# Stick-breaking scores in three rounded passes, and the order of a step around them

## The chip, the cores and the metric

One core of a Trainium2 chip runs the whole program. The metric is device time in microseconds (us), the median of several runs. The engines are TensorE (PE; its weight loads are shown apart as PEld), VectorE (DVE), ScalarE (ACT), GpSimdE (POOL) and SyncE (SP), which issues the DMAs.

## The reference

One layer on x (1 x 1024 x 1024, float32). An input projection to 5,376 columns gives q, k, v and gates of two mixers and two merge gates. Mixer A is a sliding-window attention with sinks and rotary positions. Mixer B is stick-breaking attention with 8 heads of 64 dimensions, strictly causal:

```python
z = jnp.einsum('bhtd,bshd->bhts', q_blk, k).astype(jnp.float32) * (D ** -0.5)
causal = kpos[None, :] < qpos[:, None]
log_keep = jnp.where(causal, -jax.nn.softplus(z), 0.0)
between = lax.cumsum(log_keep, axis=3, reverse=True) - log_keep
w = jnp.where(causal, jnp.exp(jax.nn.log_sigmoid(z) + between), 0.0)
return jnp.einsum('bhts,bshd->bhtd', w.astype(v.dtype), v)
```

Each mixer's output is gated with SiLU and projected up; both are merged with sigmoid gates, go through an output projection, and a LayerNorm of 1.189 x + that follows. The diff touches the first einsum (the scores z), the buffers around it and the order of the work.

## The kernel before, in words

**Products.** Features lie on partitions, time (backwards) along the free axis. Every large matrix product is made in float32r: each operand is split into a rounded part `hi` (an ACT copy into a float32r tile) and the rest `lo` (a DVE subtraction, original minus hi), and `mma3` (L214 to L216) adds three matmuls, hi by hi, hi by lo and lo by hi. The input projection has 20 pairs of weight tiles with 7 products each (`N_PRODUCTS` is 140; product q belongs to pair q // 7, position q % 7), each product being 12 matmuls of 128x128 by 128x512 into PSUM bank q % 2. Products of the later pairs are the filling between other work. After product q, ACT reads the bank (`read_bank`, L807 or L812) and rounds weights for a product three or four ahead (`part_high`, L717); DVE adds blocks (`add_block`, L1118: positions 1, 4, 5), forms sums of weights (L1127 to L1134: positions 4 and 5, two operations each) and subtracts the low parts (`low_part`, L1138: two at position 0, none at 5, one elsewhere). So a position decides how much DVE does after it: 2, 2, 1, 1, 4, 3, 1 operations for positions 0 to 6.

**Steps.** Mixer B runs in 20 steps, 5 to each pair of heads. Step s takes one or two tiles of 128 queries (`parts(s)`) that fill 1,024 score columns for each head (512 in the fifth step of a pair, which is called j = 4 below; the steps of a pair are j = 0 to 4). In PSUM the scores are four banks, z. The columns are cut where a bank ends: runs of 512+512 columns for j = 0, 512+384+128 for j = 1, 512+256+256 for j = 2, 512+128+384 for j = 3, 512 for j = 4. Key and query tiles of a pair are `ks` and `qs`, written by products well ahead.

PE's order in step s (L1612 to L1630): `values(s-2)` (L1605), `scores(s)` (L1578, float32 matmuls, one head in partitions 0 to 63 and the other in 64 to 127), `turn(s-1)` group 0 (transposes of the weights, L1593), a product, groups 1 and 2, half a product, group 3, the other half, in j = 0 the transposes of v (`turn_values`, L1559), and a third product except in j = 4.

The other engines follow with semaphores, each in its own written order. ACT: `keeps(s)` (L984, sigmoids of z; waits for the scores and for values(s-2)), copies of the turned blocks (L964), bank reads and weight roundings, and `betas(s)` (L992), which waits for the last transposes of s-1 and reads z for the last time; `scores(s+1)` waits for it. POOL cuts the diagonals (L662, L667). DVE: `gated_out(s-2)` (L1299), a scan over the first head (`break_sticks`, L1280), what follows the first product, the scan over the second head, what follows the second product, `weigh(s)` (L1288; its first piece releases group 0 of the next step's transposes), and what follows the third.

SP loads weights and stores gates and outputs. Everything else of the kernel (mixer A in a window stage before, up projection, output projection, LayerNorm behind) is not touched but for buffers and the semaphores that guard them.

Of the kernel before, what the change touches and what calls it, by code (L numbers as in the profile page):

```python
# [13 lines left out]
P = 128  # L14
SEQ = 1024
# [33 lines left out]
STEP_0 = 42  # L49
# [52 lines left out]
def halves_done(n, h):  # L102

    return 2 * h + n + 1

# [113 lines left out]
def build(nc, xt, xn, w, bias, cos, sin, sinks, ln_g, ln_b, out):  # L219
    with ExitStack() as ctx:  # L220
# [53 lines left out]
        with ExitStack() as b:  # L274
            keep0 = sb("keep0", [P, 2, SEQ], F32, b)
            keep1 = sb("keep1", [P, 2, SEQ], F32, b)
            beta = sb("beta", [P, 2, SEQ], F32, b)
            sig_g = sb("sig_g", [P, 2, HALF], F32, b)
            o_b1 = sb("o_b1", [P, SEQ], F32, b)
            v_n1 = sb("v_n1", [P, SB, P], F32, b)  # L280
            ks0, qs0 = sb("ks0", [P, SEQ], F32, b), sb("qs0", [P, SEQ], F32, b)
            v_n0 = sb("v_n0", [P, SB, P], F32, b)
            qs1, ks1 = sb("qs1", [P, SEQ], F32, b), sb("ks1", [P, SEQ], F32, b)
        qs, ks, v_n, o_b = (qs0, qs1), (ks0, ks1), (v_n0, v_n1), (o_b0, o_b1)
        keep = (keep0, keep1)

# [86 lines left out]
        def block_at(sp, m, nh):  # L373


            if sp in Q_PAIRS:
                return qa[sp][:, 8 * nh:8 * nh + 8, m, :]
            if sp in G_PAIRS:
                slot = GATE_SLOT[m, nh]
                return gate_st[:, slot, :] if slot < 2 else sw[:, slot - 2, :]  # L380
            if sp >= MG_PAIR:
# [39 lines left out]
        z_done, keep_set, beta_set = sem("z_done"), sem("keep_set"), sem("beta_set")  # L421
        keep_cut, beta_cut, scanned, w_ready = sem("keep_cut"), sem("beta_cut"), sem("scanned"), sem("w_ready")
# [34 lines left out]
        def _(sp):  # L457
# [41 lines left out]
            def merge_gate_store(i, m, nh):  # L499
                at = 4 * (i % 2) + 2 * m + nh  # L500
                if (m, nh) == (1, 0):
                    sp.wait_ge(bank_read, NP * i + 7)
                else:
                    sp.wait_ge(block_sig, 3 * (i - MG_PAIR) + BLOCKS.index((m, nh)) + 1)
                sp.dma_start(sig_d[i - MG_PAIR, m][:, half(nh)], sig_m[:, at, :]).then_inc(sig_out[at], 16)
# [12 lines left out]
            def gate_back(a):  # L518
                if a == 0:
                    for slot in GATE_SLOT.values():  # L520
                        sp.wait_ge(gate_out[slot], 16 * len(G_PAIRS))
                else:
                    sp.wait_ge(ga_set, a)
                sp.dma_start(v_t[:], gate_d[a]).then_inc(gate_in, 16)
# [160 lines left out]
        def _(act):  # L685
# [62 lines left out]
            def room(i, pos):  # L748
# [15 lines left out]
                for p in range(PAIRS):  # L764
                    if i == pair_kq(p) and pos == 0:
                        if p == 0:
                            act.wait_ge(rope_done, len(ROPE_ORDER))
                            for m in range(2):
                                act.wait_ge(gate_out[GATE_SLOT[m, 1]], 16 * len(G_PAIRS))
                        else:  # L770
                            act.wait_ge(za_done, twos)
                            if p >= 2:
                                act.wait_ge(z_done, PER_PAIR * (p - 1))
                    if i == pair_vg(p):
# [12 lines left out]
                if i == MG_PAIR and pos == 0:  # L787
                    act.wait_ge(z_done, PER_PAIR * (PAIRS - 1))
                if i == MG_PAIR + 1:
                    if pos == 0:  # L790
                        act.wait_ge(o_done, PER_PAIR * (PAIRS - 1))
                    if pos == 4:
                        act.wait_ge(z_done, STEPS)
# [27 lines left out]
            def gate_a_sigmoid(a):  # L821
                act.wait_ge(gate_in, 16 * (a + 1))
                if a == 0:
                    act.wait_ge(ob_out, 16 * (PAIRS - 1))
                else:
                    act.wait_ge(ga_mul, a)
# [28 lines left out]
            def gate_b_sigmoid(p):  # L855

                i = pair_vg(p)
                for h in range(2):
                    wait_block(act, i, 1, h)
                    if p == 0 and h == 0:  # L860
                        for k in range(2):
                            act.wait_ge(oa_out[k], 16 * NCHUNK // 4)
                    if p > 0:
                        act.wait_ge(gate_set, 2 * (p - 1) + h + 1)
                    act.activation(sig_g[:, h, :], o_b[p % 2][:, half(h)], ACT.Sigmoid).then_inc(gate_sig, 1)
# [51 lines left out]
            act.wait_ge(t_lo[4], 2)  # L917
            def exponents(c):
# [29 lines left out]
            for c in range(NCHUNK + 5):  # L948
                if c % 2 == 0 and c >= 6:
                    turned_chunk(c - 5)  # L950
                after(WINDOW_1 + c)
                if c % 2 == 0 and 4 <= c < NCHUNK + 4:
                    turned_chunk(c - 4)
                if c < NCHUNK:
                    exponents(c)

# [10 lines left out]
            def turned_values(p):  # L967

                if p == 1:
                    act.wait_ge(gate_out[GATE_SLOT[1, 0]], 16 * len(G_PAIRS))  # L970
                for g in range(2):
                    at = RING_AT["v", p, g]
                    act.wait_ge(turned, ring_count(at, False) + 1)
                    act.activation(v_n[p % 2][:, 4 * g:4 * g + 4, :].rearrange("p a d -> p (a d)"),
# [79 lines left out]
        def _(dve):  # L1054
# [86 lines left out]
            def gate_b_product(p):  # L1141

                for h in range(2):
                    o = o_b[p % 2][:, half(h)]
                    dve.wait_ge(gate_sig, 2 * p + h + 1)
                    dve.tensor_tensor(o, o, sig_g[:, h, :], ALU.mult).then_inc(gate_set, 1)
# [126 lines left out]
            outputs(twos - 1)  # L1273
# [27 lines left out]

            for s in range(STEPS):
# [112 lines left out]
        def _(pe):  # L1415
# [147 lines left out]
            def scores(s):  # L1563
# [32 lines left out]
            def values(s):  # L1596
# [4 lines left out]
                for i, (t, first, blocks) in enumerate(parts(s)):  # L1601
                    for b_ in range(blocks):
                        for h in range(2):
                            r = slice(HD * h, HD * h + HD)
                            last = pe.matmul(bank[r, P * i:P * (i + 1)], v_n[p % 2][:, t + b_, r],  # L1605
# [5 lines left out]
            half_product(2 * STEP_0)  # L1611
            for s in range(STEPS):  # L1612
                made_here = made(s)
                if s >= 2:
                    values(s - 2)
                scores(s)
                if s > 0:
                    turn(s - 1, (0,))
                    product(made_here[0])
                    turn(s - 1, (1, 2))  # L1620
                else:
                    half_product(2 * STEP_0 + 1)
# [4 lines left out]
                if s % PER_PAIR == 0:  # L1627
# [148 lines left out]
```

## Time and profile before

| | |
|---|---|
| Median of 3 runs | 734.57 us (734.19 to 734.57) |
| The profiled execution's own time | 734.3 us |
| Its span | 732.6 us, mean granted TensorE clock 0.998 |
| Busy: PE, PEld | 721.8 us (99%), 578.2 us (79%) |
| Busy: DVE, ACT, POOL | 503.1 us (69%), 398.6 us (54%), 102.5 us (14%) |
| Step stage | 174.0 to 433 us of the span, about 13.98 us a full step, 10.4 us a j = 4 step |

A matmul's busy time is longer than its share of the array, since matmuls are pipelined: distances between starts tell what one costs. The median of the runs lies 0.27 us above the profiled execution.

### The profile page before, as it was taken

What the parts mean: (1) busy time and instruction counts of PE and PEld (TensorE: products, weight loads), DVE (VectorE), ACT (ScalarE), POOL (GpSimd) and SP (SyncE); (2) the same over time, 40 slices, a digit from 0 to 9 for tenths busy, and PEclk for the clock granted to TensorE, in tenths of its full rate; (3) what the DMA queues carried; (4) which work ended last, traced back from release to release, by engine and by line L of the source; (5) the groups of instructions that cost most, each with busy time, mean ns of one, the idle gap of its engine ahead of it and who ended that gap; (6) DMA issues with size and microseconds to landing.
All of it is one profiled execution on the core that took longest, in us unless ns stands there. A gap on an engine that the chain in (4) does not pass through costs nothing.

```text
span 732.6 us, 10490 instructions
## 1 busy us (share of the span) xinstructions
PE 721.8 (99%) x3926; PEld 578.2 (79%) x3926; DVE 503.1 (69%) x721; ACT 398.6 (54%) x710; POOL 102.5 (14%) x130
## 2 busy tenths in 40 slices
PE   8999999999999999999999999999999999999995
PEld 7888877777777887777878778888877888888884
DVE  6998788756978788788777764665583456560644
ACT  6954477766665866666676764555581212240321
POOL 0000000002231321223123200000000000000782
PEclk9999999999999999999999999999999999999999
DMA  8235322231100201020012314455635343260451
GB/s 294 109 92 128 118 82 73 73 101 43 44 30 30 78 11 57 5 83 30 30 34 90 93 49 138 135 189 189 235 129 210 150 173 121 80 229 1 157 186 60
DMA packets 41491, 76.22 MB, mean 104 GB/s; under 512 B 12256, under 2 KB 16864, under 8 KB 41440
## 3 DMA queue, kind: packets, MB, share of 16 engines
q1 hardware_dynamic: 41440, 75.54, 31.0%
q8 instruction: 32, 0.52, 0.3%
q14 instruction: 19, 0.16, 0.1%
HBM read 55.07 MB, written 18.35 MB: 100 GB/s over the span
## 4 chain that ended last, share of the span: by engine, by line
PE 95%; DVE 3%; DMA 1%; ACT 0%; SPq 0%; issue 0%; ACTq 0%; DVEq 0%
PE ps L214 26%; PE ps L216 26%; PE ps L215 25%; PE ps L1578 5%; PE ps L1605 5%; PE ps L1593 5%; PE ps L1524 1%; PE ps L1536 1%; PE ps L1505 1%; DMA xr<-in_xt 1%; DVE x_lo L1157 1%; DVE t_ops L1157 1%; PE ps L1559 0%; DVE w_lo L1138 0%; DVE sig_m L1118 0%; PE ps L1493 0%
## 5 line engine op out<-in xcount | busy, mean ns | idle before, releaser
L214 PE MATMUL ps<-x_hi,w_hi 128*128 128x512 f32 x416 | 166.8, 401 | 1.3 <-DVE x_lo L1195 0.9
L216 PE MATMUL ps<-x_hi,w_lo 128*128 128x512 f32 x416 | 162.5, 391 | 0.0
L215 PE MATMUL ps<-x_lo,w_hi 128*128 128x512 f32 x416 | 162.2, 390 | 0.0
L214 PE MATMUL ps<-t_ops,w_hi 128*128 128x512 f32 x304 | 122.2, 402 | 0.6 <-DVE w_lo L1138 0.3
L1138 DVE TENSOR_TENSOR w_lo<-raw,w_hi 128x512 fp32r<-128x512 f32 x120 | 81.1, 691 | 59.3 <-ACT w_hi L717 59.2
L216 PE MATMUL ps<-t_ops,w_lo 128*128 128x512 f32 x304 | 118.7, 390 | 0.0
L215 PE MATMUL ps<-t_ops,w_hi 128*128 128x512 f32 x304 | 118.5, 390 | 0.0
L1280 DVE TENSOR_TENSOR_SCAN keep<-keep 128x895 f32<-128x895 f32 (+4 forms) x64 | 85.3, 1363 | 13.4 <-POOL keep L662 13.4
L214 PEld LDWEIGHTS ps<-x_hi,w_hi 128*128 128x128 f32 x416 | 78.4, 188 | 18.3 <-issue 2.6
L216 PEld LDWEIGHTS ps<-x_hi,w_lo 128*128 128x128 f32 x416 | 78.1, 188 | 16.9
L215 PEld LDWEIGHTS ps<-x_lo,w_hi 128*128 128x128 f32 x416 | 78.4, 188 | 14.7
L662 POOL TENSOR_SCALAR_AFFINE_SELECT keep<-keep 128x128 f32<-128x128 f32 x64 | 48.6, 778 | 280.5 <-ACT keep L984 280.5
L717 ACT ACTIVATE w_hi<-raw 128x512 fp32r<-128x512 f32 x120 | 73.5, 631 | 0.0
L216 PEld LDWEIGHTS ps<-t_ops,w_lo 128*128 128x128 f32 x304 | 57.1, 188 | 12.3
L214 PEld LDWEIGHTS ps<-t_ops,w_hi 128*128 128x128 f32 x304 | 57.1, 188 | 12.1 <-issue 0.8
L215 PEld LDWEIGHTS ps<-t_ops,w_hi 128*128 128x128 f32 x304 | 57.3, 188 | 10.6
L807 ACT ACTIVATE tmp<-ps 128x512 f32<-128x512 f32 x60 | 35.9, 599 | 44.9 <-PE ps L216 44.0
L984 ACT ACTIVATE keep<-ps 128x1023 f32<-128x1023 f32 (+1 forms) x40 | 35.4, 937 | 43.5 <-PE ps L1578 43.5
L679 POOL TENSOR_TENSOR o_t<-o_t,sig_m 128x512 f32<-128x512 f32 x14 | 18.1, 1292 | 254.9 <-ACT o_t L1049 254.9
L964 ACT ACTIVATE keep<-ps 128x512 f32<-128x512 f32 x72 | 41.2, 599 | 9.5 <-PE ps L1593 9.5
L1593 PEld LDWEIGHTS ps<-ident,beta 128*128 128x128 f32 x288 | 33.3, 141 | 14.1 <-DVE beta L1288 6.8
L1288 DVE TENSOR_TENSOR beta<-beta,keep 128x1024 f32<-128x1024 f32 (+4 forms) x48 | 43.3, 950 | 0.0
(176 smaller groups left out, 1066.8 us busy)
## 6 DMA issues: line engine op xcount, KB each, us to landing
raw<-in_w SPq DMA_DIRECT2D x28, 512.0 KB, 3.9
raw<-in_w SPq DMA_DIRECT2D x42, 256.0 KB, 2.7
sig_d<-sig_m SPq DMA_DIRECT2D x32, 256.0 KB, 3.6
sig_m<-sig_d SPq DMA_DIRECT2D x16, 512.0 KB, 4.1
xr<-in_xt SPq DMA_DIRECT2D x16, 256.0 KB, 6.0
raw<-in_xn SPq DMA_DIRECT2D x8, 512.0 KB, 3.7
out<-o_t SPq DMA_DIRECT2D x16, 256.0 KB, 2.2
o_t<-o_d SPq DMA_DIRECT2D x7, 512.0 KB, 4.8
```

Of the source, the lines that this page charges most:

```text
L214: pe.matmul(out, w_hi, x_hi, start=first, stop=False, skip_group_check=goes_on)
L215: pe.matmul(out, w_hi, x_lo, start=False, stop=False, skip_group_check=goes_on)
L216: return pe.matmul(out, w_lo, x_hi, start=False, stop=last, skip_group_check=goes_on)
L662: pool.affine_select(out=kp_d, in_=kp_d, compare_op=ALU.is_gt, fill=1.0, base=0, pattern=[[1, n]], channel_multiplier=-1).then_inc(keep_cu ...
L717: act.activation(ring_slot(w_hi, q), part_of(q), ACT.Copy).then_inc(part_hi, 1)
L964: act.activation(w_t[s % 2][:, b0:b0 + 2, :, :].rearrange("p a h t -> p (a h t)"), ps[:, 6 + at % 2, :], ACT.Copy).then_inc(turned_out, 1)
L1138: dve.tensor_tensor(ring_slot(w_lo, q), part_of(q), ring_slot(w_hi, q).bitcast(F32), ALU.subtract).then_inc(part_lo, 1)
L1280: dve.tensor_tensor_scan(stick, stick, stick, 1.0, ALU.mult, ALU.bypass).then_inc(scanned, 1)
L1288: dve.tensor_tensor(beta[:, :, first:end], beta[:, :, first:end], keep[s % 2][:, :, first - 1:end - 1], ALU.mult).then_inc(w_ready, 1)
L1578: last = pe.matmul(ps[:, 2 + 2 * h + at // HALF, at % HALF:at % HALF + m], qs[p % 2][r, P * t:P * (t + 1)], ks[p % 2][r, key:key + m], sta ...
L1593: last = pe.transpose(bank[:, at:at + P], beta[:, h, P * b_:P * (b_ + 1)], ident[:])
L1605: last = pe.matmul(bank[r, P * i:P * (i + 1)], v_n[p % 2][:, t + b_, r], w_t[s % 2][:, turned_block(first + b_), h, :], start=b_ == 0, sto ...
```

## The change

- Scores are now made as hi by hi, hi by lo, lo by hi in float32r, three passes for each run of columns and head, in place of one float32 matmul. `keys_hi` and `queries_hi` round ks and qs into `k_hi` and `q_hi` (one buffer each); `low_keys` and `low_queries` write the rest over ks and qs. The queries are done in two pieces: the first tile of 128 columns apart from the other 896 (for the first pair: in halves).
- For the next pair of heads, ACT rounds keys and first query tile in step j = 4, between the first copy of turned blocks and the first bank read; DVE subtracts in the same step, behind the second scan. The rest of the queries follows at the end of j = 4 on ACT and near the beginning of j = 0 on DVE. `scores` waits for `kq_lo` in j = 0 and j = 1.
- In each step PE issues `scores(s)` ahead of `values(s-2)`.
- Steps begin one product later (STEP_0 43 instead of 42): product 42 stands whole before step 0, and every step's products are of the next position.
- The transposes and copies of v move from j = 0 to j = 1; v_n has one buffer; the gate's sigmoid is kept in the other pair's qs; pair 13's merge gates go through o_b0 and v_t; waits guard these buffers.

```diff
-STEP_0 = 42
+STEP_0 = 43
...
-        if s < STEPS and s % PER_PAIR == 0:
+        if s < STEPS and s % PER_PAIR == 1:
             order += [("v", s // PER_PAIR, g) for g in range(2)]
...
+            def keys_hi(p):
+                wait_block(act, pair_kq(p), 0, 1)
+                if p == 0:
+                    act.wait_ge(tp_done, 4 + NCHUNK)
+                    act.wait_ge(gate_out[GATE_SLOT[1, 0]], 16 * len(G_PAIRS))
+                else:
+                    act.wait_ge(z_done, PER_PAIR * p)
+                act.activation(k_hi[:], ks[p % 2][:], ACT.Copy).then_inc(kq_hi, 1)
+
+            def queries_hi(p, at):
...
+                act.activation(q_hi[:, at], qs[p % 2][:, at], ACT.Copy).then_inc(kq_hi, 1)
...
             for c in range(NCHUNK + 5):
                 if c % 2 == 0 and c >= 6:
                     turned_chunk(c - 5)
+                if c == NCHUNK + 4:
+                    keys_hi(0)
+                    queries_hi(0, half(1))
                 after(WINDOW_1 + c)
...
+            queries_hi(0, half(0))
+            for q in range(WINDOW_1 + NCHUNK + 5, STEP_0):
+                after(q)
...
                 keeps(s)
                 if s > 0:
                     turned_blocks(s - 1, (0,))
+                last_of_pair = s % PER_PAIR == PER_PAIR - 1 and s < STEPS - 1
+                if last_of_pair:
+                    keys_hi(s // PER_PAIR + 1)
+                    queries_hi(s // PER_PAIR + 1, FIRST_TILE)
                 read_bank(made_here[0])
...
                 betas(s)
                 after(made_here[1])
+                if last_of_pair:
+                    queries_hi(s // PER_PAIR + 1, OTHER_TILES)
                 if s % PER_PAIR == 0:
+                    gate_b_sigmoid(s // PER_PAIR)
+                if s % PER_PAIR == 1:
                     turned_values(s // PER_PAIR)
-                    gate_b_sigmoid(s // PER_PAIR)
...
+            def low_keys(p):
+                dve.wait_ge(kq_hi, 3 * p + 1)
+                dve.tensor_tensor(k_lo[p % 2][:], ks[p % 2][:], k_hi[:].bitcast(F32),
+                                  ALU.subtract).then_inc(kq_lo, 1)
...
+            low_keys(0)
+            low_queries(0, half(1))
+            low_queries(0, half(0))
+            outputs(twos - 1)
...
                 if 2 <= s < STEPS - 1:
                     gated_out(s - 2)
+                if s % PER_PAIR == 0 and s > 0:
+                    low_queries(s // PER_PAIR, OTHER_TILES)
                 break_sticks(s, 0)
                 after(made_here[0])
                 break_sticks(s, 1)
+                if s % PER_PAIR == PER_PAIR - 1 and s < STEPS - 1:
+                    low_keys(s // PER_PAIR + 1)
+                    low_queries(s // PER_PAIR + 1, FIRST_TILE)
                 after(made_here[1])
                 weigh(s)
...
                 if s % PER_PAIR == 0:
-                    wait_block(pe, pair_kq(p), 0, 1)
-                    wait_block(pe, pair_kq(p), 1, 0)
+                    pe.wait_ge(kq_lo, 3 * p + (2 if p > 0 else 3))
+                if s % PER_PAIR == 1:
+                    pe.wait_ge(kq_lo, 3 * p + 3)
...
-                        for h in range(2):
-                            r = slice(HD * h, HD * h + HD)
-                            last = pe.matmul(ps[:, 2 + 2 * h + at // HALF, at % HALF:at % HALF + m],
-                                             qs[p % 2][r, P * t:P * (t + 1)], ks[p % 2][r, key:key + m],
-                                             start=True, stop=True)
+                        for i, (q_, k_) in enumerate(((q_hi, k_hi), (q_hi, k_lo[p % 2]), (q_lo[p % 2], k_hi))):
+                            for h in range(2):
+                                r = slice(HD * h, HD * h + HD)
+                                last = pe.matmul(ps[:, 2 + 2 * h + at // HALF, at % HALF:at % HALF + m],
+                                                 q_[r, P * t:P * (t + 1)], k_[r, key:key + m],
+                                                 start=i == 0, stop=i == 2)
...
             for s in range(STEPS):
                 made_here = made(s)
+                scores(s)
                 if s >= 2:
                     values(s - 2)
-                scores(s)
                 if s > 0:
                     turn(s - 1, (0,))
-                    product(made_here[0])
+                product(made_here[0])
+                if s > 0:
                     turn(s - 1, (1, 2))
-                else:
-                    half_product(2 * STEP_0 + 1)
...
-                if s % PER_PAIR == 0:
+                if s % PER_PAIR == 1:
                     turn_values(s // PER_PAIR)
```

## Rows read from the trace of the kernel before

**Rows 1.** The page: busy time of the engines, and the chain that ended last.

```profile
PE 721.8 (99%) x3926; PEld 578.2 (79%) x3926; DVE 503.1 (69%) x721; ACT 398.6 (54%) x710; POOL 102.5 (14%) x130
...
PE 95%; DVE 3%; DMA 1%; ACT 0%; SPq 0%; issue 0%; ACTq 0%; DVEq 0%
```

**Rows 2.** The chain in order of time: start us, us on the chain, what.

```profile
91.93 1.09 PE ps L1524 x16
...
261.42 1.90 PE ps L1605 x32
263.32 1.92 PE ps L1578 x12
...
291.26 1.06 PE ps L1578 x4
```

**Rows 3.** PE by line and form: busy us, mean ns; idle us.

```profile
L1578 PE MATMUL ps<-ks,qs 64*128 64x512 f32 x96 | 26.0, 632 | 0.0
...
L1578 PE MATMUL ps<-ks,qs 64*128 64x384 f32 x32 | 6.5, 483 | 0.0
...
L1578 PE MATMUL ps<-ks,qs 64*128 64x256 f32 x32 | 4.1, 376 | 0.0
L1578 PE MATMUL ps<-ks,qs 64*128 64x128 f32 x32 | 3.1, 270 | 0.0
```

**Rows 4.** Timeline of PE, 254 to 262 us: start us, us, instruction.

```profile
254.44 1.03 PE L1593 MATMUL ps<-ident,beta 128*128 128x128 f32 x8
255.23 0.48 PE L214 MATMUL ps<-t_ops,w_hi 128*128 128x512 f32 x1
...
258.53 0.39 PE L214 MATMUL ps<-x_hi,w_hi 128*128 128x512 f32 x1
...
261.03 0.39 PE L216 MATMUL ps<-x_hi,w_lo 128*128 128x512 f32 x1
```

**Rows 5.** Line L1578 alone, 263.2 to 263.6 us: count, ns, starts.

```profile
L1578 PE MATMUL ps<-ks,qs x2: 693/693/693, 263.2 to 263.3; 64*128 64x512 f32 x2
```

**Rows 6.** Timeline of step s = 9 (j = 4) and the start of s = 10.

```profile
295.50 1.03 PE L1593 MATMUL ps<-ident,beta 128*128 128x128 f32 x8
...
296.19 1.09 ACT L964 ACTIVATE keep<-ps 128x512 f32<-128x512 f32 x2
...
298.14 1.21 DVE L1280 TENSOR_TENSOR_SCAN keep<-keep 128x511 f32<-128x511 f32 x1
...
298.89 1.02 ACT L992 ACTIVATE beta<-ps 128x1024 f32<-128x1024 f32 x1
299.69 1.97 PE L1605 MATMUL ps<-keep,v_n 128*64 128x128 f32 x32
```

**Rows 7.** ACT and DVE by line and form: busy us, mean ns; idle us and releaser.

```profile
L717 ACT ACTIVATE w_hi<-raw 128x512 fp32r<-128x512 f32 x120 | 73.5, 631 | 0.0
...
L1138 DVE TENSOR_TENSOR w_lo<-raw,w_hi 128x512 fp32r<-128x512 f32 x120 | 81.1, 691 | 59.3 <-ACT w_hi L717 59.2
...
L1328 DVE TENSOR_TENSOR w_lo<-raw,w_hi 128x1024 fp32r<-128x1024 f32 x5 | 6.1, 1221 | 1.9 <-ACT w_hi L699 1.9
```

**Rows 8.** Timeline of the last product of the window stage and step 0.

```profile
171.38 0.69 ACT L812 ACTIVATE qs<-ps,bias_c 128x512 f32<-128x512 f32 x1 [2.12 <-PE ps L216]
...
172.43 0.50 PE L214 MATMUL ps<-x_hi,w_hi 128*128 128x512 f32 x1
172.60 1.28 ACT L984 ACT_TABLE_LOAD   x1
...
184.54 2.35 DVE L1288 TENSOR_TENSOR beta<-beta,keep 128x1024 f32<-128x1024 f32 x2
...
185.81 0.66 PE L1593 MATMUL ps<-ident,beta 128*128 128x128 f32 x4
```

**Rows 9.** Timeline of step s = 6 (j = 1): its keeps, and weigh in the next step.

```profile
251.31 1.94 ACT L984 ACTIVATE keep<-ps 128x1023 f32<-128x1023 f32 x2 [1.69 <-PE ps L1578]
...
262.93 2.41 DVE L1288 TENSOR_TENSOR beta<-beta,keep 128x1024 f32<-128x1024 f32 x3
```

More of the change, by code:

```diff
@@ L104, in halves_done @@
     return 2 * h + n + 1
+FIRST_TILE, OTHER_TILES = slice(0, P), slice(P, SEQ)
 def first_piece(i):
@@ L277, in build, with sig_g @@
             beta = sb("beta", [P, 2, SEQ], F32, b)
-            sig_g = sb("sig_g", [P, 2, HALF], F32, b)
+            v_n = sb("v_n", [P, SB, P], F32, b)
             o_b1 = sb("o_b1", [P, SEQ], F32, b)
-            v_n1 = sb("v_n1", [P, SB, P], F32, b)
+            k_hi = sb("k_hi", [P, SEQ], F32R, b)
             ks0, qs0 = sb("ks0", [P, SEQ], F32, b), sb("qs0", [P, SEQ], F32, b)
-            v_n0 = sb("v_n0", [P, SB, P], F32, b)
+            q_hi = sb("q_hi", [P, SEQ], F32R, b)
             qs1, ks1 = sb("qs1", [P, SEQ], F32, b), sb("ks1", [P, SEQ], F32, b)
-        qs, ks, v_n, o_b = (qs0, qs1), (ks0, ks1), (v_n0, v_n1), (o_b0, o_b1)
+        with ExitStack() as low:
+            sb("below_low", [P, 9, SEQ], F32, low)
+            k_lo0, q_lo0 = sb("k_lo0", [P, SEQ], F32R, low), sb("q_lo0", [P, SEQ], F32R, low)
+            sb("between_low", [P, SEQ], F32, low)
+            q_lo1, k_lo1 = sb("q_lo1", [P, SEQ], F32R, low), sb("k_lo1", [P, SEQ], F32R, low)
+        qs, ks, o_b = (qs0, qs1), (ks0, ks1), (o_b0, o_b1)
+        q_lo, k_lo = (q_lo0, q_lo1), (k_lo0, k_lo1)
         keep = (keep0, keep1)
+        def sig_g(p):
+            return halves(qs[(p + 1) % 2])
         w_t = [k[:].rearrange("p h t -> p (h t)").rearrange("p (k h t) -> p k h t", h=2, t=P) for k in keep]
@@ L380, in block_at @@
                 return gate_st[:, slot, :] if slot < 2 else sw[:, slot - 2, :]
+            if sp == MG_PAIR + 1:
+                return (o_b0 if m else v_t)[:, half(nh)]
             if sp >= MG_PAIR:
@@ L504, in merge_gate_store @@
                     sp.wait_ge(block_sig, 3 * (i - MG_PAIR) + BLOCKS.index((m, nh)) + 1)
-                sp.dma_start(sig_d[i - MG_PAIR, m][:, half(nh)], sig_m[:, at, :]).then_inc(sig_out[at], 16)
+                sp.dma_start(sig_d[i - MG_PAIR, m][:, half(nh)], block_at(i, m, nh)).then_inc(sig_out[at], 16)
             def output_back(k):
@@ L521, in gate_back @@
                         sp.wait_ge(gate_out[slot], 16 * len(G_PAIRS))
+                    for nh in range(2):
+                        sp.wait_ge(sig_out[4 + nh], 16)
                 else:
@@ L773, in room @@
                                 act.wait_ge(z_done, PER_PAIR * (p - 1))
+                    if i == pair_kq(p) and pos == 4 and p > 0:
+                        act.wait_ge(gate_set, 2 * p)
                     if i == pair_vg(p):
@@ L788, in room @@
                     act.wait_ge(z_done, PER_PAIR * (PAIRS - 1))
+                if i == MG_PAIR and pos == 4:
+                    act.wait_ge(gate_set, 2 * PAIRS)
                 if i == MG_PAIR + 1:
                     if pos == 0:
-                        act.wait_ge(o_done, PER_PAIR * (PAIRS - 1))
+                        act.wait_ge(turned, ring_count(RING_AT["v", PAIRS - 1, 1], False) + 1)
                     if pos == 4:
-                        act.wait_ge(z_done, STEPS)
+                        act.wait_ge(ob_out, 16 * (PAIRS - 1))
+                if i == MG_PAIR + 3 and pos == 0:
+                    act.wait_ge(z_done, STEPS)
                 if i >= MG_PAIR + 2:
@@ L823, in gate_a_sigmoid @@
                 if a == 0:
-                    act.wait_ge(ob_out, 16 * (PAIRS - 1))
+                    for nh in range(2):
+                        act.wait_ge(sig_out[6 + nh], 16)
                 else:
@@ L859, in gate_b_sigmoid @@
                     wait_block(act, i, 1, h)
[L860 to L865, printed above, removed]
+                    if p == 0:
+                        act.wait_ge(za_done, twos)
+                    else:
+                        act.wait_ge(z_done, PER_PAIR * p)
+                    act.activation(sig_g(p)[:, h, :], o_b[p % 2][:, half(h)], ACT.Sigmoid).then_inc(gate_sig, 1)
             def after(q):
@@ L917, in _ @@
             act.wait_ge(t_lo[4], 2)
+            def keys_hi(p):
+                wait_block(act, pair_kq(p), 0, 1)
+                if p == 0:
+                    act.wait_ge(tp_done, 4 + NCHUNK)
+                    act.wait_ge(gate_out[GATE_SLOT[1, 0]], 16 * len(G_PAIRS))
+                else:
+                    act.wait_ge(z_done, PER_PAIR * p)
+                act.activation(k_hi[:], ks[p % 2][:], ACT.Copy).then_inc(kq_hi, 1)
+            def queries_hi(p, at):
+                wait_block(act, pair_kq(p), 1, at.start // HALF)
+                if at == OTHER_TILES:
+                    wait_block(act, pair_kq(p), 1, 1)
+                if p == 0:
+                    act.wait_ge(za_done, twos)
+                act.activation(q_hi[:, at], qs[p % 2][:, at], ACT.Copy).then_inc(kq_hi, 1)
             def exponents(c):
@@ L955, in _ @@
                     exponents(c)
+            queries_hi(0, half(0))
+            for q in range(WINDOW_1 + NCHUNK + 5, STEP_0):
+                after(q)
             def turned_blocks(s, groups):
@@ L967, in turned_values @@
             def turned_values(p):
-                if p == 1:
-                    act.wait_ge(gate_out[GATE_SLOT[1, 0]], 16 * len(G_PAIRS))
+                if p == 0:
+                    for k in range(2):
+                        act.wait_ge(oa_out[k], 16 * NCHUNK // 4)
+                else:
+                    act.wait_ge(o_done, PER_PAIR * p)
                 for g in range(2):
@@ L1272, in _, with low_queries @@
                 after(WINDOW_1 + c)
-            outputs(twos - 1)
+            def low_keys(p):
+                dve.wait_ge(kq_hi, 3 * p + 1)
+                dve.tensor_tensor(k_lo[p % 2][:], ks[p % 2][:], k_hi[:].bitcast(F32),
+                                  ALU.subtract).then_inc(kq_lo, 1)
+            def low_queries(p, at):
+                dve.wait_ge(kq_hi, 3 * p + (2 if at in (half(1), FIRST_TILE) else 3))
+                dve.tensor_tensor(q_lo[p % 2][:, at], qs[p % 2][:, at], q_hi[:, at].bitcast(F32),
+                                  ALU.subtract).then_inc(kq_lo, 1)
             def break_sticks(s, h):
@@ L1300, in gated_out @@
                                       ALU.mult).then_inc(o_set, 1)
+            low_keys(0)
+            low_queries(0, half(1))
+            low_queries(0, half(0))
+            outputs(twos - 1)
+            for q in range(WINDOW_1 + NCHUNK + 5, STEP_0):
+                after(q)
             for s in range(STEPS):
@@ L1604, in values @@
                             r = slice(HD * h, HD * h + HD)
-                            last = pe.matmul(bank[r, P * i:P * (i + 1)], v_n[p % 2][:, t + b_, r],
+                            last = pe.matmul(bank[r, P * i:P * (i + 1)], v_n[:, t + b_, r],
                                              w_t[s % 2][:, turned_block(first + b_), h, :],
@@ L1608, in values @@
                 last.then_inc(o_done, 1)
-            half_product(2 * STEP_0)
+            for q in range(WINDOW_1 + NCHUNK + 5, STEP_0):
+                product(q)
             for s in range(STEPS):
                 made_here = made(s)
+                scores(s)
                 if s >= 2:
                     values(s - 2)
-                scores(s)
                 if s > 0:
                     turn(s - 1, (0,))
-                    product(made_here[0])
+                product(made_here[0])
+                if s > 0:
                     turn(s - 1, (1, 2))
-                else:
-                    half_product(2 * STEP_0 + 1)
                 half_product(2 * made_here[1])
```

5 lines of the change are left out of this document (3 added, 2 removed).

## Prediction

> **What bounds the kernel now.** I read the page first: busy time and the chain that ended last. PE is busy 99% of the span, and 95% of the chain is PE work [rows 1]. So every microsecond put on or taken off PE's own stream counts whole, and other engines count only where PE would have to wait for them. The chain in order of time then shows how a step is built, with PE blocks end to end: values 1.90 us, scores 1.92 us (1.06 us in j = 4), and the transposes follow at once [rows 2]. L1578 shows no idle time by form [rows 3]. I therefore add up two things: what the scores cost PE, and which wait of PE is new.
>
> **Scores, the gain.** The forms of L1578 give 96 x 512 + 32 x 384 + 32 x 256 + 32 x 128 = 73,728 columns in 192 records [rows 3], two records to a matmul. The two heads run side by side: of the 512-column records two start within 0.1 us, and no third in the first 0.4 us [rows 5]. A record then takes two cycles a column and a matmul four: a full block is 1,024 columns x 4 / 2.4 = 1.71 us at the 2.4 GHz clock (the granted share is 0.998), and of its 1.92 us [rows 2] 0.21 is left for its ends. For the 16 full and 4 half steps that is 18,432 columns x 4 / 2.4 = 30.7 us. Three passes at one cycle a column are 23.0 us: 7.7 us less, if the two heads still overlap.
>
> Against this, a float32r matmul of 512 columns stands 0.227 us after the last one (258.53 to 261.03 us is 11 of them), not 0.213 [rows 4]. There will be 48 runs of columns x 3 = 144 passes; at 0.014 us each that is 2.0 us back. And the 24 passes of 128 columns are short (0.053 us of columns): eight transposes with 128-column weights take 0.79 us, 0.10 each, and 16 records of 64x128 take 1.09 us with the block's ends, so a pair of them no more than 0.14 [rows 2, 4]. I take 0.12 us a pass: 24 x (0.12 - 0.067) = 1.3 us back. Gain: 7.7 - 2.0 - 1.3 = 4.4 us. Bounds, while heads overlap: with no 0.014 and 0.107 a short pass, 7.7 - 24 x 0.054 = 6.4 us; with a short pass at the float32 matmul's four cycles a column (0.213), 7.7 - 2.0 - 24 x 0.146 = 2.2 us.
>
> The Trainium skill, TensorE: Matmul & The Clock Gate, section LDWEIGHTS (loading the stationary operand), gives a load as columns / 1.2 ns, which for 128 columns is 107 ns; the transposes' 0.10 us agrees. By it a short pass would be 0.107 us and the gain 0.3 us larger.
>
> **Edits of order that cost nothing by themselves.** Scores ahead of values: the number of blocks and of changes between them stays; keeps(s) waits for values(s-2) as well, so it starts where it did against the next transposes. The scores now come 1.9 us sooner after betas. In full steps betas is done well before, since a whole product stands behind the half that follows its release; in j = 4 it ends at 298.89 + 1.02 = 299.91 against a start of scores at 299.69 [rows 6], a wait of 0.2 to 0.3 us, which hides under the larger one below. Transposes of v a step later: the same instructions on PE; j = 1 grows by them, and DVE gets more time there. Moved stores, guards and buffers: PE waits for none of them, as the blocks they guard are whole steps old. SP's order gains nothing but product 42's entry.
>
> **New wait 1: keys and first queries of the next pair (3 times).** In j = 4 low_keys stands behind the second scan, and that behind the low part of a product's weights, for which ACT must first read a bank, copy two turned groups and round. The transposes start at 295.50 and ACT's copies of them at 296.19 [rows 6], now 0.09 us later, since position 6 is read with the L812 form (0.69 in rows 8, L807 takes 0.60). They end at 297.37, then rounding 0.63 to 297.93, low part 0.69 to 298.60 (instructions of one engine overlap by some 0.06), scan 1.21 to 299.77, low keys 1.22 to 300.93, first query tile (128 columns; I take 0.2, a quarter of L1138's columns) to 301.1 [rows 6, 7]. PE is ready at 299.69, so it stands 1.4 us. This is anchored in PE's own transposes of that step: a faster score block doesn't shorten it. 3 x 1.4 = 4.2 us. Bounds: six handovers, each up to 0.05 us shorter or longer than I take them, give 1.1 to 1.7 a time.
>
> **New wait 2: step 0 (once).** Low keys and both halves of the queries stand on DVE behind the low part that follows the read of product 41 and ends at 171.38 + 0.69 + 0.57 + 0.69 = 173.3 [rows 7, 8]: 173.3 + 1.2 + 0.6 + 0.6 = 175.7, while product 42, begun at 172.43, ends at 175.2: 0.5 us. Then ACT must treat product 42 (a read and two roundings, to 177.2) and load its table (1.28 us, formerly in idle time) ahead of keeps: 178.4 in place of 176.05. Weigh came 8.5 us behind keeps; with one DVE operation fewer, 7.9: 186.3, first piece done 187.5. PE comes to the transposes at 177.2 + 3 x 2.73 + 1.5 = 187.0: 0.5 us. Before, these two met within 0.1 us (184.54 + 1.22 against 185.81) [rows 8]. Together 1.0, bounds 0.2 to 1.8.
>
> **New wait 3: j = 3 to j = 4 (4 times).** With steps a product later, j = 3 gets position 4 as second product, with four DVE operations ahead of weigh. That is what j = 1 has now: weigh 262.93 - 251.31 = 11.62 us after keeps, first piece at 12.84 [rows 9]. PE comes to the transposes of j = 4 10.0 (rest of the step) + 0.89 (half a score block) + 1.90 = 12.8 after: 0.1 us each, 0.4 in all, bounds 0 to 1.2. In j = 4 itself and j = 0 DVE has the added 2.5 us a pair, of which all but the 1.4 above lies beside PE work.
>
> **Sum.** 4.2 + 1.0 + 0.4 = 5.6 us of waits less 4.4 us of scores is 1.2 us more. Against the profiled execution (span 732.6, time 734.3) that is 735.5; on the median, 0.27 higher, 735.8.
>
> **Rivals.** (B) Narrow passes at float32's rate: the float32r pass may not keep one cycle a column at 128 columns. Nothing before shows a float32r matmul under 512 columns, so nothing speaks against it. Gain 2.2 instead of 4.4: 738.0.
> (C) The block's ends get cheaper, and it is faster. Of the 1.92 us, 0.21 are not columns, while product to values costs only 261.42 - 261.26 or about 0.1 [rows 2, 4]. If the float32r block pays 0.1 in place of 0.21 (20 x 0.11 = 2.2 us) and, with one head's load beside the other's columns, not the 0.014 either (2.0 us), the gain is 8.6 and the time 734.57 + 5.6 - 8.6 = 731.6. It decides from a gain over 5.6. For it: the float32 score blocks' 1.71 us of columns leave no room for 0.014 a record in their middle [rows 2]. Against: every float32r product pays it [rows 4], and values, with other operands, pay 0.19 at their ends too.
> (D) The heads don't run side by side in float32r. Then 18,432 x 3 x 2 / 2.4 = 46.1 us, plus 288 x 0.014 = 4.0 and 48 short passes x 0.053 = 2.5, in place of 30.7: 21.9 us more, with waits of 4.7: 761.2. For it: no float32r matmul of 64 rows is in the trace. Against: the float32 ones overlap, by partitions alone.
> That the change doesn't do what it says isn't likely: the instructions are written out.
>
> **How the numbers follow.** Forecast 0.46, with its own range 733.8 to 737.5; B 0.16; C 0.21; D 0.12; others 0.05. The range 731.5 to 739.5 takes in the forecast, B and C and leaves D out. A measurement of this kernel tells changes over about 0.2%, 1.5 us, from none: under 733.1 is faster, over 736.04 slower. The forecast's own cases are half within that and two fifths above; with B and D above and C mostly below: faster 0.26, same 0.29, slower 0.45.
>
> **What would show it.** Right: PE idle before L1578's successor of about 1.4 us at s = 5, 10 and 15, released by DVE's low queries; about 0.5 us at step 0 and at the first transposes; a full score block of 1.45 to 1.55 us. B: 128-column passes over 0.2 us apart, so steps j = 1 and j = 3 with longer blocks than j = 0. C: blocks of 1.4 us or less. D: blocks of about 2.8 us. I would be wrong if DVE reaches low_keys before PE's last half product in j = 4, or if heads part.

## The result, and the profile after

| | before | after |
|---|---|---|
| Median, 12 runs each | 734.49 us | 736.58 us |
| Ratio, 95% interval | | 1.0026 (1.0018 to 1.0035) |
| Profiled execution, span | 732.6 us | 734.9 us |
| PE, DVE, ACT busy | 721.8, 503.1, 398.6 us | 717.9, 516.1, 407.6 us |

The change makes the kernel 0.26% slower. The page after, read like [rows 1] (busy time, then the chain by engine), shows PE with less work (3.9 us) and a chain that is PE's for 87% of the span in place of 95%:

```profile
PE 717.9 (98%) x4022; PEld 584.8 (80%) x4022; DVE 516.1 (70%) x733; ACT 407.6 (55%) x722; POOL 103.2 (14%) x130
...
PE 87%; DVE 8%; ACT 2%; issue 2%; DMA 1%; SPq 0%; POOL 0%; ACTq 0%; POOLq 0%; DVEq 0%
```

The score blocks on the chain in order of time (start us, us), which answer to [rows 2]: steps j = 2, j = 3, then j = 1 and j = 2 of the next pair. They took 1.92 us each before:

```profile
198.83 1.60 PE ps L1662 x15
...
212.51 1.75 PE ps L1662 x15
...
251.36 1.71 PE ps L1662 x18
...
265.18 1.60 PE ps L1662 x15
```

From start of block to start of the next one, the blocks are 1.58, 1.71, 1.60, 1.76 and 0.89 us for j = 0 to 4, 7.54 a pair against 4 x 1.92 + 1.06 = 8.74: 4.8 us less in all. PE by line and form (busy us, mean ns; idle us and releaser) answers to [rows 3]: of the three passes only the first has idle time before it, 4.8 us in four waits for q_lo.

```profile
L1662 PE MATMUL ps<-k_hi,q_hi 64*128 64x512 f32 x48 | 11.7, 475 | 4.8 <-DVE q_lo L1343 4.8
L1662 PE MATMUL ps<-k_hi,q_lo 64*128 64x512 f32 x48 | 9.6, 391 | 0.0
...
L1662 PE MATMUL ps<-k_lo,q_hi 64*128 64x128 f32 x16 | 2.2, 271 | 0.0
```

Step s = 4 (j = 4) and the start of s = 5, the timeline that answers to [rows 6]:

```profile
227.83 2.42 DVE L1359 TENSOR_TENSOR beta<-beta,keep 128x1024 f32<-128x1024 f32 x3
...
230.65 1.07 ACT L955 ACTIVATE k_hi<-ks 128x1024 fp32r<-128x1024 f32 x1
...
232.17 0.47 DVE L1370 TENSOR_TENSOR o_b<-o_b,ps 128x128 f32<-128x128 f32 x2
...
232.78 1.06 PE L1677 MATMUL ps<-ident,beta 128*128 128x128 f32 x8 [0.27 <-DVE o_b L1370]
233.45 1.09 ACT L1017 ACTIVATE keep<-ps 128x512 f32<-128x512 f32 x2 [0.21 <-PE ps L1677]
234.42 0.64 ACT L741 ACTIVATE w_hi<-w_x 128x512 fp32r<-128x512 f32 x1
...
235.09 0.69 DVE L1201 TENSOR_TENSOR w_lo<-w_x,w_hi 128x512 fp32r<-128x512 f32 x1 [1.32 <-ACT w_hi L741]
235.70 1.22 DVE L1351 TENSOR_TENSOR_SCAN keep<-keep 128x511 f32<-128x511 f32 x1
...
236.21 1.02 ACT L1048 ACTIVATE beta<-ps 128x1024 f32<-128x1024 f32 x1
236.83 1.20 DVE L1338 TENSOR_TENSOR k_lo<-ks,k_hi 128x1024 fp32r<-128x1024 f32 x1
...
237.94 0.49 DVE L1343 TENSOR_TENSOR q_lo<-qs,q_hi 128x128 fp32r<-128x128 f32 x1
...
238.58 0.50 PE L1662 MATMUL ps<-k_hi,q_hi 64*128 64x512 f32 x2 [1.51 <-DVE q_lo L1343]
```

Two waits of PE are to be seen. At 238.58 the first scores of the next pair have waited for the low queries; the half product before them, with the wait, takes 3.15 us where it took 1.57, so 1.58 us. At 232.78 the transposes of group 1 have waited for DVE to empty the values' PSUM bank: the product before them takes 3.26 us in place of 2.84, 0.43 us with a rounding. (The idle time in brackets is less than that, since the last matmul's modelled end runs into it.) Both stand at all three pair changes. In step 0:

```profile
174.39 1.29 DVE L1343 TENSOR_TENSOR q_lo<-qs,q_hi 128x512 fp32r<-128x512 f32 x2
175.74 0.50 PE L1662 MATMUL ps<-k_hi,q_hi 64*128 64x512 f32 x2 [0.26 <-DVE q_lo L1343]
177.26 1.28 ACT L1040 ACT_TABLE_LOAD   x1
187.76 0.55 PE L1677 MATMUL ps<-ident,beta 128*128 128x128 f32 x3 [0.23 <-DVE beta L1359]
```

The second score block takes 2.02 us instead of 1.71. Product 42 takes 3.27 us, from its first start at 172.47 to that of the scores. Without a wait it takes 2.95, as the later run with all edits shows (start of its first matmul, then of the scores, with no idle time before them):

```profile
172.80 0.50 PE L218 MATMUL ps<-x_hi,w_hi 128*128 128x512 f32 x1
...
175.75 0.49 PE L1664 MATMUL ps<-k_hi,q_hi 64*128 64x512 f32 x2
```

So step 0 waits 0.3 us at its scores and 0.3 us at the transposes.

The sum by PE's starts: 3 x 1.58 + 3 x 0.43 + 0.62 in step 0 + 4 x 0.07 at the first transposes of j = 4 + 3 x 0.03 at those of groups 1 and 2 = 7.0 us of waits, less 4.8 us of scores, is 2.2 us. The spans differ by 2.3, the medians by 2.1.

### The profile page after: what moved, and what is told of

It is laid out like the page before. It is cut to its first block, busy times and chain, and to the rows that moved or that the text cites. A ratio compares the mean times of both kernels' runs of the same rounds, so it can differ in the third digit from the quotient of the medians.

```text
span 734.9 us, 10725 instructions
## 1 busy us (share of the span) xinstructions
PE 717.9 (98%) x4022; PEld 584.8 (80%) x4022; DVE 516.1 (70%) x733; ACT 407.6 (55%) x722; POOL 103.2 (14%) x130
## 4 chain that ended last, share of the span: by engine, by line
PE 87%; DVE 8%; ACT 2%; issue 2%; DMA 1%; SPq 0%; POOL 0%; ACTq 0%; POOLq 0%; DVEq 0%
PE ps L218 24%; PE ps L220 24%; PE ps L219 24%; PE ps L1677 4%; PE ps L1689 4%; PE ps L1662 3%; PE ps L1606 1%; PE ps L1618 1%; DVE beta L1359 1%; PE ps L1587 1%; DVE keep L1351 1%; DVE w_lo L1201 1%; DMA xr<-in_xt 1%; DVE x_lo L1220 1%; DVE t_ops L1220 1%
## 5 line engine op out<-in xcount | busy, mean ns | idle before, releaser
L686 POOL TENSOR_SCALAR_AFFINE_SELECT keep<-keep 128x128 f32<-128x128 f32 x64 | 44.8, 716 | 282.7 <-ACT keep L1040 282.5
L1677 PE MATMUL ps<-ident,beta 128*128 128x128 f32 x288 | 41.5, 276 | 1.1 <-DVE o_b L1370 0.8
```

The source lines that it names most:

```text
L686: pool.affine_select(out=kp_d, in_=kp_d, compare_op=ALU.is_gt, fill=1.0, base=0, pattern=[[1, n]], channel_multiplier=-1).then_inc(keep_cu ...
L1677: last = pe.transpose(bank[:, at:at + P], beta[:, h, P * b_:P * (b_ + 1)], ident[:])
```

## The experiments

The time of before is 734.45 us for the first four runs, 734.37 us for the next four and 734.28 us for the last three. Where no edit is named, a kernel is the changed one.

**Low keys sooner.** On DVE, in j = 4:

```diff
                 break_sticks(s, 0)
+                if s % PER_PAIR == PER_PAIR - 1 and s < STEPS - 1:
+                    low_keys(s // PER_PAIR + 1)
+                    low_queries(s // PER_PAIR + 1, FIRST_TILE)
                 after(made_here[0])
                 break_sticks(s, 1)
-                if s % PER_PAIR == PER_PAIR - 1 and s < STEPS - 1:
-                    low_keys(s // PER_PAIR + 1)
-                    low_queries(s // PER_PAIR + 1, FIRST_TILE)
```

> Edit: in step j = 4 DVE subtracts the low keys and first queries of the next pair directly behind its first scan, ahead of what follows the first product, where it stood idle 1.3 us for a rounding on ACT. Theory (the added time is PE waiting for DVE's low queries behind the second scan): the wait of 1.58 us at the first scores of pairs 2 to 4 falls to about 0.3 us, where the score banks' last reader (betas on ACT) takes its place; 3 x 1.3 = 3.8 us less than the changed kernel, about 732.7 us. Rival (the time went into the passes themselves, or ACT's own rounding is what comes last): the same wait, 736.6 us.

Measured: 732.96 us, 0.9981 of before (0.9972 to 0.9991). The timeline shows the low keys in DVE's idle time, the same low part and second scan as before behind them, and the scores now released by ACT's last read of their banks (betas):

```profile
232.69 1.21 DVE L1351 TENSOR_TENSOR_SCAN keep<-keep 128x511 f32<-128x511 f32 x1
233.82 1.19 DVE L1338 TENSOR_TENSOR k_lo<-ks,k_hi 128x1024 fp32r<-128x1024 f32 x1
234.94 0.28 DVE L1343 TENSOR_TENSOR q_lo<-qs,q_hi 128x128 fp32r<-128x128 f32 x1
235.21 0.69 DVE L1201 TENSOR_TENSOR w_lo<-w_x,w_hi 128x512 fp32r<-128x512 f32 x1
...
236.32 1.02 ACT L1048 ACTIVATE beta<-ps 128x1024 f32<-128x1024 f32 x1
...
237.39 0.50 PE L1662 MATMUL ps<-k_hi,q_hi 64*128 64x512 f32 x2 [0.22 <-ACT beta L1048]
```

The wait is 0.27 us (1.84 against 1.57) in place of 1.58. The theory holds; the place of two instructions in DVE's queue was worth 3.6 us.

**Values gated sooner.** On DVE, for the steps before j = 4:

```diff
-                if 2 <= s < STEPS - 1:
+                if 2 <= s < STEPS - 1 and s % PER_PAIR != PER_PAIR - 1:
                     gated_out(s - 2)
...
                 weigh(s)
...
-                if s == STEPS - 2:
-
+                if s % PER_PAIR == PER_PAIR - 2:
                     gated_out(s - 1)
```

> Edit: in step j = 3 DVE gates the values of j = 2 between weigh and what follows the third product, not at the start of the next step. Theory (the transposes of group 1 in j = 4 wait 0.43 us for a PSUM bank that DVE empties late, since j = 3 now ends with more DVE work): these three waits go and the wait at the next scores, anchored at the same transposes, stays 1.58 us; 1.3 us less than the changed kernel, 735.3 us. Rival (a wait that is given back at the next scores, because DVE is late anyway by a fixed time): the wait of 0.43 us goes and the 1.58 us grows to 2.0 us, 736.6 us.

Measured: 735.83 us, 1.0018 (1.0009 to 1.0026), 0.75 us less than the changed kernel. The wait of 0.43 us is gone, but that at the scores grew to 1.74 (3.31 less 1.57):

```profile
238.57 0.51 PE L1661 MATMUL ps<-k_hi,q_hi 64*128 64x512 f32 x2 [1.67 <-DVE q_lo L1343]
```

Neither theory holds whole: a little over a third of what was removed came back, 0.16 us. ACT's order accounts for most of it. In the changed kernel ACT reads the product's bank (232.55 to 233.24 us) mostly while PE stands, and its copies of the turned groups start 0.67 us after PE's transposes (233.45 against 232.78). Without that wait the copies stand behind the read and start 0.78 us after (233.44 against 232.66).

**Values first.** On PE:

```diff
-                scores(s)
                 if s >= 2:
                     values(s - 2)
+                scores(s)
```

> Edit: values(s-2) ahead of scores(s) again, as before; all else as in the changed kernel. Theory (the scores come 1.9 us sooner than their operands in j = 0): PE does the 1.9 us of values while DVE finishes, so the wait of 1.58 us goes whole and the others stay; 3 x 1.58 = 4.7 us less than the changed kernel, 731.8 us, faster than before. Rival (scores ahead of values let keeps start sooner and the later steps gain by it): steps grow elsewhere and the time is 736 us or more.

Measured: 732.96 us, 0.9981 (0.9972 to 0.9989). The 1.58 us went whole, as expected; 0.35 us came in its place (3 times), one block later, since weigh of j = 4 stands behind the same DVE work:

```profile
240.80 0.33 PE L1677 MATMUL ps<-ident,beta 128*128 128x128 f32 x1 [0.28 <-DVE beta L1359]
```

So 3.6 us less and not 4.7. It is the reversed order that lets the late operands stop PE, and nothing speaks for the rival (that later steps gain by it). What weigh stands behind is tested in the run with weigh sooner.

**The order alone.** Float32 scores from ks and qs, no rounding or subtraction of them; new order, steps a product later, and the moved transposes of v and buffers as in the change (excerpt):

```diff
-                        for i, (q_, k_) in enumerate(((q_hi, k_hi), (q_hi, k_lo[p % 2]), (q_lo[p % 2], k_hi))):
+                        for i, (q_, k_) in enumerate(((qs[p % 2], ks[p % 2]),)):
...
-                                                 start=i == 0, stop=i == 2)
+                                                 start=True, stop=True)
```

> Edit: float32 scores as before, without any rounding or subtraction of keys and queries, in the new order and with steps a product later. Theory: the order by itself costs the bank wait of group 1 (0.43 us less the 0.17 us that a float32 block is longer, 3 times), a new wait of 0.25 us for betas at the first scores of three pairs, and nothing else: 734.5 + 0.8 + 0.8 = 736.1 us. Rival (order costs nothing, only the split operands do): 734.5 us.

Measured: 736.37 us, 1.0025 (1.0016 to 1.0034). Both small waits are there, 0.35 us for the bank and 0.28 us for betas, three times each:

```profile
232.97 0.30 PE L1658 MATMUL ps<-ident,beta 128*128 128x128 f32 x1 [0.20 <-DVE o_b L1360]
...
237.47 0.70 PE L1643 MATMUL ps<-ks,qs 64*128 64x512 f32 x2 [0.21 <-ACT beta L1044]
```

The order and the later start cost 1.9 us by themselves, nearly as much as the whole change. The other runs tell them apart: the wait for betas goes with values first, the wait for the bank with step 42. The bank wait stands here without any splitting of keys and queries.

**Step 42.** `STEP_0 = 42`, nothing else.

> Edit: STEP_0 is 42 again in the changed kernel; scores stay ahead of values and in three passes. Theory (the later product moves DVE work into j = 3 and so causes the bank wait in j = 4, but gives the first split its time): the waits of 0.43, 0.07 and 0.03 us go three times (1.5 us less), and step 0 waits 3.2 us for its operands in place of 0.8 us; 736.5 + 2.4 - 1.5 = 737.4 us. Rival (the later product is harmless in the steps): 736.5 + 2.4 = 738.9 us.

Measured: 738.81 us, 1.0060 (1.0047 to 1.0074). Step 0 waits 3.2 us as worked out and the bank wait in j = 4 is gone, but the time is 1.4 us over the theory's, close to the rival's for another reason. By stretch (busy us and count of each engine, then the granted clock and DMA), PE comes out of that wait at half its clock (0.50 is the 1.2 GHz level); it fell while PE still stood:

```profile
172.00:175.70 3.70, 0.53 (x4) 0.07 (x4) 3.06 (x5) 2.41 (x4) 0.00 (x0) 0.85 0.00 0
175.70:178.60 2.90, 2.87 (x13) 1.85 (x13) 0.57 (x1) 0.00 (x0) 0.00 (x0) 0.50 0.31 90
178.60:182.00 3.40, 3.40 (x11) 2.73 (x10) 1.81 (x1) 1.94 (x2) 1.51 (x2) 0.59 0.00 0
182.00:186.00 4.00, 4.00 (x19) 3.30 (x19) 2.30 (x4) 3.06 (x4) 0.56 (x1) 1.00 0.00 0
```

The first score block takes 2.86 us instead of 1.58 and the products behind it 9.68 instead of 8.42: 2.5 us, the price of the 1.2 GHz level in this execution. That is more than the 1.4 us, but the wait at the pairs fell from 1.58 to 1.34 us as well, which the theory didn't have, and the profiled execution (739.43 us) is one of the slower of the five (738.26 to 739.78).

**Passes alone.** Values first and `STEP_0 = 42` together.

> Edit: values ahead of scores and STEP_0 42, so of the change only the three passes with their splitting are left (and the moved transposes of v). Theory: 4.8 us less in score blocks; 3.2 us of waiting at step 0 and 0.35 us at the first transposes of three pairs more: 734.5 - 4.8 + 3.2 + 1.05 = 733.9 us. Rival (the three passes bring nothing net, the gain of the run with values first is from the later product): 734.5 us or more.

Measured: 734.47 us, 1.0005 (0.9996 to 1.0014): no change, the number of the rival. The trace gives the theory's parts and one more: blocks 4.8 us shorter, 3.2 us of waiting at step 0, 0.2 us at the first transposes, none for weigh in j = 0, and a lower clock after the wait. That makes the first score block 1.92 us instead of 1.59 and the products behind it 9.65 instead of 8.42, 1.6 us in all. The same stretches as in the last table:

```profile
172.00:175.70 3.70, 0.50 (x6) 0.05 (x4) 3.12 (x5) 2.35 (x4) 0.00 (x0) 1.00 0.00 0
175.70:178.60 2.90, 2.90 (x14) 1.85 (x15) 0.51 (x1) 0.90 (x1) 0.00 (x0) 0.70 0.31 90
```

The passes do bring 4.8 us; step 0 takes it all back (3.2 + 0.2 + 1.6). One product more ahead of step 0 covers that wait and keeps the clock up, which is what the later start is worth.

**All mended.** The first two edits, and for step 0 (excerpt):

```diff
+                if c == NCHUNK + 4:
+                    low_keys(0)
+                    low_queries(0, half(1))
                 after(WINDOW_1 + c)
...
             queries_hi(0, half(0))
+            act.activation(small[:, 6, 7:8], bias_c[:, 0:1], ACT.Sigmoid)
```

> Edits, all at once: low keys and first queries behind the first scan; values of j = 2 gated in j = 3; for step 0 the low keys and half the low queries ahead of what follows product 41, and a one-column sigmoid on ACT that loads the table before product 42 ends. Theory: the first edit leaves 0.27 us at betas (3 times), the second now takes off its full 0.43 us (3 times), since the next scores no longer wait for DVE, and the third takes off 0.8 us: 732.96 - 1.3 - 0.8 = 730.9 us. Rival (the waits are given back by the next one on the path): 732.5 us or more.

Measured: 731.23 us, 0.9957 (0.9944 to 0.9969). The table loads at 173.49 us, ahead of product 42's read, and neither wait of step 0 is left. The time is 0.3 us over the theory's, which took 0.8 us for step 0 where 0.6 was to be had. No run has the one-column sigmoid without the earlier subtractions, so what each is worth is not shown. What stays at the pairs is betas, with 0.28 us of PE's time (1.85 against 1.57):

```profile
236.60 0.50 PE L1664 MATMUL ps<-k_hi,q_hi 64*128 64x512 f32 x2 [0.21 <-ACT beta L1049]
```

**All mended, values first.**

> The edits of the run with all of them, and values ahead of scores as before. Theory: no wait for betas (0.27 us, 3 times) and, since DVE is earlier, no wait for weigh in j = 0: 730.9 - 0.8 = 730.1 us. Rival (with the DVE mended, the order of scores and values makes no difference): 730.9 us.

Measured: 731.31 us, 0.9957 (0.9944 to 0.9969). The wait for betas went and 0.34 us for weigh took its place, so the rival is right that the order makes no difference here (731.31 against 731.23 us): one wait takes the place of another.

**Weigh sooner.** That kernel, and in j = 4 `weigh(s)` ahead of `after(made_here[1])` on DVE.

> Edit: the run with all edits and values first, and in j = 4 weigh ahead of the two low parts that follow the second product. Theory (the 0.34 us at the first transposes of j = 0 are weigh standing behind two low parts that wait for ACT): three such waits go, 731.3 - 1.0 = 730.3 us. Rival (the low parts then come late for their products, or POOL's cut of beta comes last): 731.3 us or more.

Measured: 729.73 us, 0.9937 (0.9923 to 0.9950), the fastest: 4.55 us under before, against 4.8 us that the blocks are shorter. The three waits for weigh are gone, as expected. The time is 0.6 us under the theory's; in the profiles 0.6 us of the difference to the last run lies ahead of step 0 (first scores at 175.07 against 175.68 us), which the edit doesn't touch, and its cause stays open. No run has this edit with scores first. The chain is PE's again for as much as before the change:

```profile
PE 95%; DVE 3%; DMA 1%; SPq 0%; ACT 0%; issue 0%; ACTq 0%; DVEq 0%
```

**Heads apart.** The two loops around the matmul exchanged, so that three passes of one head stand ahead of three of the other.

> Edit: in each run of columns the three passes of the first head stand ahead of the three of the second, so neighbours in PE's queue use the same rows; all else as in the changed kernel. Theory (two heads overlap only because neighbouring matmuls use different rows, and order is kept): a j = 0 block goes from 1.58 to about 2.6 us (four or five of six matmuls of a run one after the other) and the time to 750 us or more. Rival (PE overlaps them whatever their order): blocks stay 1.58 us, 736.6 us.

Measured, a single run: 736.83 us and blocks of 1.59, 1.72, 1.61, 1.76 and 0.89 us. The first matmul of the second head, fourth in the program, starts with the first one (count, ns, first and last start in us, of one block):

```profile
L1662 PE MATMUL ps<-k_hi,q_hi x2: 492/492/492, 265.2 to 265.3; 64*128 64x512 f32 x2
...
L1662 PE MATMUL ps<-k_lo,q_hi x2: 387/387/387, 265.6 to 265.6; 64*128 64x512 f32 x2
```

The theory is wrong and the rival right: the heads overlap in either order, over this distance. Whether PE itself brings the fourth matmul forward, or the order was changed before it reached PE, this run can't tell.

**Short runs.** `m = P` in `scores`: 128 columns a run everywhere.

> Edit: every run of score columns is cut into runs of 128 columns, so a j = 0 block is 24 short passes for each head in place of 6 long ones; all else as in the changed kernel. Theory (a short float32r pass of 64 rows takes about 0.10 us, set by its weight load): a j = 0 block takes 0.21 + 24 x 0.10 = 2.6 us, a j = 4 block 1.4 us. Rival (a short pass runs at float32's four cycles a column, 0.213 us): 5.3 us.

Measured, a single run: 764.17 us; a j = 0 block takes 2.82 us, so a short pass (2.82 - 0.21) / 24 = 0.109 us, and a j = 4 block 1.49 us:

```profile
176.04 0.33 PE L1662 MATMUL ps<-k_hi,q_hi 64*128 64x128 f32 x2 [0.26 <-DVE q_lo L1343]
176.20 0.28 PE L1662 MATMUL ps<-k_lo,q_hi 64*128 64x128 f32 x2
176.31 0.27 PE L1662 MATMUL ps<-k_hi,q_lo 64*128 64x128 f32 x2
176.43 0.27 PE L1662 MATMUL ps<-k_hi,q_hi 64*128 64x128 f32 x2
```

That is near the theory's rate and half of the rival's 0.213. It is also twice the 0.053 us that 128 columns take at one cycle a column. That its weight load sets the rate, as the theory says, fits but isn't shown. The time also has three stretches at the 1.2 GHz level in it (last section).

## Why the prediction was right

It said 735.8 us, 1.2 us more than before, from 5.6 us of waits less 4.4 us of scores. Measured: 2.1 us more, from about 7.0 less 4.8. The mechanism is the one forecast, late operands at the pair changes against shorter score blocks. That the number came so close is in part luck: a wait of 1.3 us was left out, and a larger gain and a smaller wait at step 0 made up for much of it.

- **Score blocks.** Right in mechanism: the heads overlap, a long pass stands 0.23 us from the next, a block's ends cost 0.21 us. j = 0 by that is 1.28 + 6 x 0.014 + 0.21 = 1.57, measured 1.58; j = 2 is 1.62, measured 1.60. Mis-sized was the short pass, taken as 0.12 us: 0.109 in a row of them, about 0.10 in the blocks of j = 1 and 0.115 in those of j = 3 (worked out like the above). That is most of why the gain is 4.8 and not 4.4. B, C and D fall with it: the short runs rule out B, blocks of 1.58 us C, and the two heads' common starts D. The 0.1 us that C takes from 261.42 - 261.26 is 0.16 as written; by the timeline values start at 261.35, which gives the 0.1.
- **Wait 1.** Right in place, cause and size: 1.58 us against 1.4, three times. "A faster score block doesn't shorten it" fits the one run that changes the block's length with this wait in place: with short runs the j = 4 block is 0.60 us longer, and the wait is 1.72 us (3.29 less 1.57), not shorter. The wait for betas that was said to hide under the larger one is there too, 0.28 us, both with float32 scores and with the low keys sooner. What the text left out is that this wait exists only because scores stand ahead of values: it listed that edit under those that cost nothing by themselves, while values first took 3.6 us off.
- **Wait 2.** 0.3 us in place of 0.5 at the scores, 0.3 in place of 0.5 at the transposes. DVE was done when worked out: scores start 3.27 us after product 42 in both. But PE reaches them after 2.95 us and not 2.75; the change from product to score block, 0.2 us, was left out.
- **Wait 3.** 0.07 us a time for 0.1.
- **What failed.** The step "New wait 3: j = 3 to j = 4": the four DVE operations ahead of weigh in j = 3 were priced for weigh only, 0.1 us each. But DVE gates the values (`gated_out`, 232.17 us above) behind that same weigh (227.83) and what follows the third product, so it empties the values' bank late, and group 1 waits for it, 0.43 us three times. The wait comes from the later start and not from the splitting: it stands in the run with the order alone, and goes with step 42 or with values gated sooner. That 1.3 us is more than the 0.8 us by which the time was missed. I followed weigh through DVE's queue and not the gating that stands behind it. The step "Edits of order that cost nothing by themselves" failed too: the order and the later start cost 1.9 us by themselves, the bank wait and the one for betas.

## What to carry to other kernels

When a step's operands come from another engine's queue, find for each the place in that queue and ask what it stands behind: here two DVE instructions, moved ahead of one that waits for ACT, turned 0.26% slower into 0.2% faster. An issue order that brings work forward on the busiest engine takes away the time in which other engines could finish what that work waits for. Follow every semaphore of the late engine, not only the one that came to mind, since each operation behind the late one is late too.

## What was not expected of the hardware

- TensorE's clock: in the run with step 42, PE stood 3.2 us, from about 172.5 to 175.7. The granted clock was 1.00 before, has a mean of 0.85 over 172.0 to 175.7, was 0.50 (the 1.2 GHz level) when PE came back and 1.00 again from 182 us on. Passes of 512 columns were 0.43 us apart at the lower level and not 0.23. With the same standstill, the run with the passes alone kept 1.00 until PE was back and fell only then (0.70 in 175.7 to 178.6). So the same wait cost 2.5 us in one execution and 1.6 in the other. Waits of 1.58 us a pair left the clock at 1.00 in the changed kernel. In the kernel of short runs the waits are as long, 1.65 us of idle time, but short passes follow them, and there the clock fell behind each of the three; why it fell there and not in the changed kernel, no run tells. The first of the three, then the stretches around it:

```profile
243.44 0.33 PE L1662 MATMUL ps<-k_hi,q_hi 64*128 64x128 f32 x2 [1.65 <-DVE q_lo L1343]
```

```profile
240.00:243.40 3.40, 1.79 (x10) 1.18 (x8) 3.40 (x5) 2.96 (x5) 1.14 (x1) 1.00 0.00 0
243.40:248.10 4.70, 4.66 (x50) 4.57 (x50) 2.23 (x3) 1.00 (x2) 0.00 (x0) 0.59 0.16 56
```

- Matmuls on different rows start within 0.1 us of each other even when two others on the first one's rows stand between them in the program (the run with heads apart).
- Part of a short wait can be given back: of 0.43 us removed 0.27 us was gained, since ACT had used most of the pause.
